# Second block: the 31 taps of one channel tile of a depthwise convolution, on VectorE or on GpSimd

## The chip, the core and the metric

The kernel is one program on one core of a Trainium2 chip. The metric is the device time of one launch in microseconds (us): lower is better. Engines are named as the profile names them: PE (TensorE), PEld (its weight loads), DVE (VectorE), ACT (ScalarE), POOL (GpSimd), SP (SyncE, which issues most DMAs).

## The reference, cut to what matters

The model has a first block and a second block of two layers, for 256 tokens of width 1024. A layer of the second block is a mixer, a cross-attention to a memory of 256 tokens, and a feed-forward part (dense in the first layer, a mixture of eight experts in the second). The mixer:

```python
z = xn @ w_in
a_val, a_gate, b_gate, c_gate, b_in, c_z = jnp.split(z, splits, axis=-1)
ya = a_val * jax.nn.sigmoid(a_gate)                        # 384 channels
ya = causal_depthwise_conv(ya, conv_a_w) + conv_a_b        # 31 taps
ya = jax.nn.silu(layernorm(ya, ln_a_g, ln_a_b))
yb = b_gate * causal_depthwise_conv(c_gate * b_in, conv_b_w)   # 3 taps
c_u, c_v = jnp.split(jax.nn.gelu(c_z), 2, axis=-1)
c_v = layernorm(c_v, ln_c_g, ln_c_b)
yc = chunk_spatial_gate(c_u, c_v, gmlp_ws, gmlp_b)
y = rmsnorm of jnp.concatenate([ya, yb, yc]) by groups of 64
return y @ w_mix_out
```

The change concerns the second line of `ya`: per channel, 31 shifted copies of a row of 256 tokens, each times one weight, are added to a bias.

## The kernel before

Channels lie on the 128 partitions, tokens along the row. Branch A has 384 channels, so three tiles t = 0, 1, 2 of 128x256 in `yap` (with 30 zeros before each row); their convolution is summed in `y8[:, t]`. Both are views of the tile `arena`, which is the name that the profile shows. `vb` holds v of branch C, `prod` and `cg` serve branch B.

**Weights.** SP loads each weight slot of 128x2048 float32 into `raw`. ACT rounds it to `whi` (L612, in `ahead`), DVE computes the rest `wlo = raw - whi` (L1578, in `ahead`), and PE makes three products of each (L1045, 48 matmuls per group of 256 columns). `whi` and `wlo` have three buffers, so a slot's rounding waits until PE has used the slot three before. In `group(g)` ACT and DVE first split up to two slots ahead, then wait for PE's product of g. The order of all work is written out by hand in each engine's program; no planner sets it.

**The mixer of a layer, by engine.** PE multiplies the groups mixa (three), mix_bg, mix_bgcg, then turns the memory (L1303), mix_cg, mix_bin, mix_binuv, mix_u, mix_v. Then come small products between the groups of keys (xk0 to xk3) and values (xv0 to xv3) of the memory: the means of v (L1319 to L1321), keys 0, the sums of squares of v, keys 1, v turned (L1331), keys 2, the spatial weights turned (L1337), the spatial product (L1345), keys 3, then the means of branch A (L1352, which waits at L1350 for all 93 taps), values 0, its squares (L1357), values 1, the squares of the whole mix (L1363), values 2, and so on.

DVE runs the taps between its splits. `conv_a(n)` issues the next n of a list ordered by k, then t. The first of each tile is a TENSOR_SCALAR (L1922), the others are a SCALAR_TENSOR_TENSOR (L1926), which reads a shifted row of `yap` and `y8`, both in SBUF, and writes `y8`. A tap waits for the tap of its own tile before it, three places back. Nine taps follow the splits of each of mix_bg, mix_bgcg, mix_cg, mix_bin, mix_u and mix_v; nine more follow `memory_low("xk", 0)`, then 12, 12 and 6 follow the low parts of keys 1, 2 and 3 (93 in all). In between lie:

- L1932, L1934: the memory scaled by its norm; L1942: the memory's low part, eight instructions, with one input in PSUM and one in SBUF
- L1947, L1952: the products for branch B, with one input in PSUM
- L1967: v centred, once L1321 has given its mean, and ACT's square of it (L882), behind which ACT splits xk2
- L1972, L1974, L1977: v normed and scaled; PE's L1331 waits for L1977
- `memory_low` (its instruction is L1596): the low parts of keys and values
- after the last tap: L1991 to L1994 (branch B), L2002 and L2003 (branch C), then L2007 (branch A centred, by the means of L1352), L2011, L2013. ACT squares (L898), applies silu (L905) and squares everything (L909), for which PE's L1363 waits.

POOL has little to do in this stretch. Per layer it clears the pads (L566, L567), loads the memory (L570), waits for PE to have turned it, loads the spatial weights `wsl` (L573), waits for them and clears a corner (L576, which PE's L1337 needs), waits for L1977 and loads the biases `gb` (L583), which DVE's L2002 needs.

Of the kernel before, what the change touches and what calls it, by code (L numbers as in the profile page):

```python
# [15 lines left out]
T = 256  # L16
# [170 lines left out]
def build_program(nc, w, onehot, out, bias_dram):  # L187
# [51 lines left out]
    with ctx:  # L239
# [235 lines left out]
        def _(pool):  # L475
# [88 lines left out]
            for l in range(2):  # L564
                pool.wait_ge(sem("dve_read"), reads_at[stage_groups[("down", "down2")[l]][-1]])
                link(pool.memset(yap[:, :, 0:30], 0.0))  # L566
                pool.memset(prod[:, :, 0:2], 0.0).then_inc(sem("mix_padded"), 1)  # L567
# [4 lines left out]
                pool.wait_ge(sem("mem_turned"), 4 * (l + 1))  # L572
                pool.dma_start(wsl, w["gmlp_ws_2"][l].rearrange("g i j -> i g j")).then_inc(sem("ws_landed"), 16)  # L573
                pool.wait_ge(sem("ws_landed"), 16 * (l + 1))
                pool.wait_ge(sem("mix_padded"), l + 1)
                pool.memset(wsl[0:64, :, 64:128], 0.0).then_inc(sem("ws_masked"), 1)  # L576
# [463 lines left out]
        def _(pe):  # L1040
# [250 lines left out]
            for l in range(2):  # L1291
# [58 lines left out]
                pe.wait_ge(sem("conv_taps"), 93 * (l + 1))  # L1350
# [211 lines left out]
        def _(dve):  # L1562
# [343 lines left out]
            for l in range(2):  # L1906
                norm(f"mix{l}", xT, lambda c: col("norm_mix_g_2", DC * l + c))
                dve.wait_ge(sem("mix_padded"), l + 1)
# [7 lines left out]
                taps = [(k, t) for k in range(TAPS_A) for t in range(3)]  # L1916
                done = {"k": 0}

                def conv_a(n):
                    for k, t in taps[done["k"]:done["k"] + n]:  # L1920
                        if k == 0:
                            ins = dve.tensor_scalar(y8[:, t], yap[:, t, 0:T], vec[:, aw + t:aw + t + 1], vec[:, ab + t:ab + t + 1],  # L1922
                                                    ALU.mult, ALU.add)
                        else:
                            dve.wait_ge(sem("conv_taps"), 93 * l + 3 * k + t - 2)
                            ins = dve.scalar_tensor_tensor(y8[:, t], yap[:, t, k:k + T], vec[:, aw + 3 * k + t:aw + 3 * k + t + 1],  # L1926
                                                           y8[:, t], ALU.mult, ALU.add)
                        ins.then_inc(sem("conv_taps"), 1)
                    done["k"] += n
# [5 lines left out]
                for stage in ("mix_bg", "mix_bgcg", "mix_cg"):  # L1935
                    ahead_of(stage_groups[f"{stage}{l}"][0])
                    conv_a(9)
# [10 lines left out]
                conv_a(9)  # L1948
# [4 lines left out]
                for stage in ("mix_u", "mix_v"):  # L1953
                    ahead_of(stage_groups[f"{stage}{l}"][0])
                    conv_a(9)
# [14 lines left out]
                conv_a(9)  # L1970
# [8 lines left out]
                conv_a(12)  # L1979
                memory_low("xk", 2)  # L1980
                conv_a(12)
                memory_low("xk", 3)
                conv_a(93 - done["k"])
                dve.wait_ge(sem("conv_taps"), 93 * (l + 1))
# [255 lines left out]
```

## Time and profile before

| | us |
|---|---|
| median of three runs (2370.57 to 2370.88) | 2370.84 |
| the profiled execution | 2369.96 |
| its span, first to last instruction | 2368.2 |
| PE busy | 2232.5 |
| DVE busy | 1749.6 |
| ACT busy | 1328.3 |
| POOL busy | 75.8 |

The mean granted clock of TensorE is 0.973 of its full speed. Times below are from the span's start. The mixer of the first layer lies between about 599 and 735 us, that of the second between about 1050 and 1187 us; the code of both is the same. In a timeline a row gives the start, the time of the group, the engine, the line and operation, output and input, and in brackets the engine's idle time ahead of it and what ended it.

### The profile page before, as it was taken

The page shows a single profiled execution, that of the slowest core. Times are in us where ns is not written, and L with a number is a line of the kernel's source. Part 1 is how long each engine was busy: PE and PEld are TensorE (multiplying, and loading weights), DVE is VectorE, ACT ScalarE, POOL GpSimd, SP SyncE. Part 2 cuts the span into 40 slices and gives each one's busy share as a digit, 9 for nine tenths or more (in the row PEclk, how much of TensorE's full clock was granted, in tenths as well). Part 3 has the DMA queues.
Part 4 walks back from the last instruction along what each step waited for, and adds up shares of the span by engine and source line. Part 5 has one row for each costly group of instructions (what it writes and reads, how often), then busy time and mean ns, then how long its engine had stood idle before and what let it go on. Part 6 is the DMA issues. An engine that isn't in the chain of part 4 may idle for free.

```text
span 2368.2 us, 35018 instructions
## 1 busy us (share of the span) xinstructions
PE 2232.5 (94%) x13975; PEld 1997.1 (84%) x13975; DVE 1749.6 (74%) x1928; ACT 1328.3 (56%) x1288; POOL 75.8 (3%) x159
## 2 busy tenths in 40 slices
PE   6999998999989899999897799999999999999997
PEld 4988987999978899999787688888888888888886
DVE  5668855884795555558864588888888888888885
ACT  3564433653534444345343576777676777777674
POOL 5011200000000000000000000000000000000000
PEclk9999999999999999999899799999999999999998
DMA  9637746756544356555342499989999999989992
GB/s 274 181 122 228 238 156 167 197 175 187 160 134 143 90 144 188 172 177 164 114 163 82 159 374 338 372 321 371 336 367 347 347 374 335 369 318 374 333 368 110
DMA packets 415499, 566.51 MB, mean 239 GB/s; under 512 B 17098, under 2 KB 268212, under 8 KB 415344
## 3 DMA queue, kind: packets, MB, share of 16 engines
q1 hardware_dynamic: 410160, 556.31, 68.8%
q0 software_dynamic: 4896, 6.89, 1.2%
q8 instruction: 121, 1.98, 0.3%
q10 hardware_dynamic: 288, 1.05, 0.1%
q14 instruction: 34, 0.28, 0.0%
HBM read 562.37 MB, written 1.84 MB: 238 GB/s over the span
## 4 chain that ended last, share of the span: by engine, by line
PE 80%; DVE 9%; ACT 4%; issue 2%; DMA 0%; ACTq 0%; SPq 0%; DVEq 0%
PE pair L1045 58%; PE misc L1045 13%; DVE wlo L1578 2%; DVE arena L1926 2%; PE misc L1451 1%; PE pair L1462 1%; PE misc L1486 1%; ACT whi L612 1%; PE misc L1115 1%; PE misc L1230 1%; PE misc L1099 0%; PE misc L1363 0%; DVE rt L1603 0%; DMA raw<-in_w_up_dram 0%; PE misc L1271 0%
## 5 line engine op out<-in xcount | busy, mean ns | idle before, releaser
L2122 DVE TENSOR_TENSOR wlo<-raw,whi 128x2048 fp32r<-128x2048 f32 x338 | 769.8, 2289 | 124.4 <-ACT whi L976 123.4
L976 ACT CAST whi<-raw 128x2048 fp32r<-128x2048 f32 x338 | 646.9, 1917 | 202.8 <-PE misc L1045 101.2
L1045 PE MATMUL pair<-hh,whi 128*128 128x256 f32 x1840 | 532.4, 289 | 24.0 <-DVE hl L1596 19.6
L1578 DVE TENSOR_TENSOR wlo<-raw,whi 128x2048 fp32r<-128x2048 f32 (+1 forms) x174 | 385.1, 2215 | 210.6 <-ACT whi L612 209.9
L1045 PE MATMUL pair<-hl,whi 128*128 128x256 f32 x1840 | 526.5, 286 | 0.0
L1045 PE MATMUL pair<-hh,wlo 128*128 128x256 f32 x1840 | 526.2, 286 | 0.0
L1045 PE MATMUL pair<-whi,oph 128*128 128x512 f32 (+1 forms) x1024 | 394.4, 385 | 4.8 <-DVE wlo L2122 3.1
L1045 PE MATMUL pair<-wlo,oph 128*128 128x512 f32 (+1 forms) x1024 | 386.6, 378 | 0.0
L1045 PE MATMUL pair<-whi,opl 128*128 128x512 f32 (+1 forms) x1024 | 385.9, 377 | 0.0
L1045 PEld LDWEIGHTS pair<-hh,whi 128*128 128x128 f32 x1840 | 359.3, 195 | 30.9 <-issue 26.4
L612 ACT CAST whi<-raw 128x2048 fp32r<-128x2048 f32 (+1 forms) x174 | 320.6, 1843 | 87.4 <-PE pair L1045 72.9
L1045 PEld LDWEIGHTS pair<-hl,whi 128*128 128x128 f32 x1840 | 359.5, 195 | 0.3
L1045 PEld LDWEIGHTS pair<-hh,wlo 128*128 128x128 f32 x1840 | 359.2, 195 | 0.0
L1045 PEld LDWEIGHTS pair<-whi,oph 128*128 128x128 f32 x1024 | 193.7, 189 | 42.6 <-DVE wlo L2122 6.1
L1045 PEld LDWEIGHTS pair<-wlo,oph 128*128 128x128 f32 x1024 | 193.4, 189 | 36.2
L1045 PEld LDWEIGHTS pair<-whi,opl 128*128 128x128 f32 x1024 | 193.9, 189 | 33.4
L1045 PE MATMUL pair<-oph,whi 128*128 128x256 f32 x672 | 194.1, 289 | 5.0 <-issue 3.0
L1045 PE MATMUL pair<-opl,whi 128*128 128x256 f32 x672 | 190.8, 284 | 0.0
L1045 PE MATMUL pair<-oph,wlo 128*128 128x256 f32 x672 | 190.8, 284 | 0.0
L1045 PE MATMUL misc<-whi,oph 128*128 128x512 f32 x448 | 176.1, 393 | 0.0
L1045 PE MATMUL misc<-wlo,oph 128*128 128x512 f32 x448 | 174.5, 389 | 0.0
L1045 PE MATMUL misc<-whi,opl 128*128 128x512 f32 x448 | 174.3, 389 | 0.0
(418 smaller groups left out, 2502.1 us busy)
## 6 DMA issues: line engine op xcount, KB each, us to landing
raw<-in_moe_w_gate_dram SPq DMA_DIRECT2D x114, 1024.0 KB, 7.0
raw<-in_moe_w_up_dram SPq DMA_DIRECT2D x112, 1024.0 KB, 7.0
raw<-in_moe_w_down_dram SPq DMA_DIRECT2D x112, 1024.0 KB, 6.8
raw<-in_w_in_dram SPq DMA_DIRECT2D x38, 1024.0 KB, 5.3
raw<-in_w_mod_dram SPq DMA_DIRECT2D x24, 1024.0 KB, 5.9
raw<-in_w_up_dram SPq DMA_DIRECT2D x44, 512.0 KB, 5.2
raw<-in_w_xkv_dram SPq DMA_DIRECT2D x16, 1024.0 KB, 5.5
raw<-in_ffn_w_gate_dram SPq DMA_DIRECT2D x22, 512.0 KB, 3.9
```

The lines of the kernel that those rows point to most:

```text
L612: act.copy(whi[:, i_ % SPLIT, 0:size], raw[:, raw_of(n), 0:size]).then_inc(sem("hi_ready"), 1)
L976: act.copy(whi[:, q, :], raw[:, r, :]).then_inc(sem("hi_ready"), 1)
L1045: ins = pe.matmul(out_, lhs, rhs, start=start and i == 0, stop=stop and i == 2)
L1115: ins = pe.matmul(misc[:, 0, 0:T], ones[:], squares[:, c], start=(c == 0), stop=(c == DC - 1))
L1230: ins = pe.matmul(misc[:, h % 2, i * P:(i + 1) * P], q[:, qb * P:(qb + 1) * P], k[:, kb * P:(kb + 1) * P], start=True, stop=True)
L1451: ins = pe.matmul(misc[:, 1 - half, c * P:(c + 1) * P], hn_tok[:, i, f:f + P], place[:, i, :], start=(i == 0), stop=(i == 1))
L1462: ins = pe.matmul(banks[:, r, m * T:(m + 1) * T], ye[:, f:f + P], comb_t[:, cb], start=True, stop=True)
L1486: ins = pe.transpose(misc[:, bank, c * P:(c + 1) * P], sh[:, j % 2, c * P:(c + 1) * P], ident[:])
L1578: dve.tensor_tensor(wlo[:, i_ % SPLIT, 0:size], raw[:, raw_of(n), 0:size], whi[:, i_ % SPLIT, 0:size].bitcast(F32), ALU.subtract).then_inc ...
L1926: ins = dve.scalar_tensor_tensor(y8[:, t], yap[:, t, k:k + T], vec[:, aw + 3 * k + t:aw + 3 * k + t + 1], y8[:, t], ALU.mult, ALU.add)
L2122: dve.tensor_tensor(wlo[:, q, :], raw[:, r, :], whi[:, q, :].bitcast(F32), ALU.subtract).then_inc(sem("lo_ready"), 1)
```

## The change

Tile 2 of the convolution leaves DVE. DVE's list then holds 62 taps instead of 93 (`range(2)`), each waiting for the tap two places back, and its nine, nine, ..., 12, 12, 6 become six, six, ..., 8, 8, 4. POOL computes tile 2: for k = 0 a tensor_scalar into `y8[:, 2]`, for each k from 1 to 30 a tensor_scalar (multiply) into a scratch row and a tensor_tensor that adds it to `y8[:, 2]`, 61 instructions per layer, each waiting for the one before it through `link`. The scratch row lies in a part of `raw` that holds no weights at that time. POOL's load of `wsl` stands ahead of tap 10, its wait and the clearing ahead of tap 14; the loads of `gb` stay behind the last tap. PE's means of branch A wait for DVE's 62 taps and for POOL. The semaphore `mix_padded` is replaced by `pool_mixed`, which counts two per layer.

```diff
@@ POOL
-                pool.memset(prod[:, :, 0:2], 0.0).then_inc(sem("mix_padded"), 1)
+                pool.memset(prod[:, :, 0:2], 0.0).then_inc(sem("pool_mixed"), 1)
...
-                pool.wait_ge(sem("mem_turned"), 4 * (l + 1))
-                pool.dma_start(wsl, w["gmlp_ws_2"][l].rearrange("g i j -> i g j")).then_inc(sem("ws_landed"), 16)
-                pool.wait_ge(sem("ws_landed"), 16 * (l + 1))
-                pool.wait_ge(sem("mix_padded"), l + 1)
-                pool.memset(wsl[0:64, :, 64:128], 0.0).then_inc(sem("ws_masked"), 1)
+                aw, ab = VROW["conv_a_w_2"] + 93 * l, VROW["conv_a_b_2"] + 3 * l
+                pool.wait_ge(sem("dve_read"), reads_at[stage_groups[f"mixa{l}"][2]])
+                link(pool.tensor_scalar(y8[:, 2], yap[:, 2, 0:T], vec[:, aw + 2:aw + 3], vec[:, ab + 2:ab + 3], ALU.mult, ALU.add))
+                for k in range(1, TAPS_A):
+                    if k == 10:
+                        pool.wait_ge(sem("mem_turned"), 4 * (l + 1))
+                        pool.dma_start(wsl, w["gmlp_ws_2"][l].rearrange("g i j -> i g j")).then_inc(sem("ws_landed"), 16)
+                    if k == 14:
+                        pool.wait_ge(sem("ws_landed"), 16 * (l + 1))
+                        pool.wait_ge(sem("pool_mixed"), 2 * l + 1)
+                        pool.memset(wsl[0:64, :, 64:128], 0.0).then_inc(sem("ws_masked"), 1)
+                    tap = spare[:, 0:T]
+                    link(pool.tensor_scalar(tap, yap[:, 2, k:k + T], vec[:, aw + 3 * k + 2:aw + 3 * k + 3], None, ALU.mult))
+                    ins = pool.tensor_tensor(y8[:, 2], y8[:, 2], tap, ALU.add)
+                    if k < TAPS_A - 1:
+                        link(ins)
+                ins.then_inc(sem("pool_mixed"), 1)
@@ PE
-                pe.wait_ge(sem("conv_taps"), 93 * (l + 1))
+                pe.wait_ge(sem("conv_taps"), 2 * TAPS_A * (l + 1))
+                pe.wait_ge(sem("pool_mixed"), 2 * (l + 1))
@@ DVE
-                taps = [(k, t) for k in range(TAPS_A) for t in range(3)]
+                taps = [(k, t) for k in range(TAPS_A) for t in range(2)]
...
-                            dve.wait_ge(sem("conv_taps"), 93 * l + 3 * k + t - 2)
+                            dve.wait_ge(sem("conv_taps"), 2 * TAPS_A * l + 2 * k + t - 1)
...
-                    conv_a(9)
+                    conv_a(6)
...
-                conv_a(12)
+                conv_a(8)
...
-                conv_a(93 - done["k"])
-                dve.wait_ge(sem("conv_taps"), 93 * (l + 1))
+                conv_a(2 * TAPS_A - done["k"])
+                dve.wait_ge(sem("conv_taps"), 2 * TAPS_A * (l + 1))
```

## Rows read from the trace of the kernel before

**Rows 1.** The stages of both mixers: us, busy (instructions), PE's clock, DMA share, GB/s

```profile
625.00:650.00 25.00, 25.00 (x213) 25.00 (x212) 24.88 (x46) 13.57 (x19) 1.25 (x2) 1.00 0.49 148
...
600.00:760.00 160.00, 147.53 (x1119) 142.54 (x1119) 125.57 (x204) 74.61 (x88) 4.64 (x8) 0.95 0.45 143
1050.00:1212.00 162.00, 149.69 (x1131) 145.05 (x1132) 127.24 (x208) 77.03 (x92) 5.56 (x9) 0.94 0.45 144
```

**Rows 2.** Waits from 600 to 730 us: total, times, longest

```profile
PE misc L1352 <- DVE arena L1926: 3.8, 1, 3.8
...
PE misc L1331 <- DVE arena L1977: 3.0, 1, 3.0
```

**Rows 3.** Timeline of DVE in the first mixer

```profile
623.45 0.17 DVE L1932 RECIPROCAL tiny<-tiny 128x2 f32<-128x2 f32 x1 [3.26 <-ACT tiny L847]
...
638.71 3.65 DVE L1926 SCALAR_TENSOR_TENSOR arena<-arena,vec 128x256 f32<-128x256 f32 x9
642.28 3.22 DVE L1942 SCALAR_TENSOR_TENSOR opl<-misc,vec,oph 128x256 fp32r<-128x256 f32 x8
...
651.77 2.28 DVE L1578 TENSOR_TENSOR wlo<-raw,whi 128x2048 fp32r<-128x2048 f32 x1
...
665.84 1.08 DVE L1967 SCALAR_TENSOR_TENSOR arena<-misc,arena 128x256 f32<-128x256 f32 x3
669.63 2.29 DVE L1578 TENSOR_TENSOR wlo<-raw,whi 128x2048 fp32r<-128x2048 f32 x1 [2.71 <-ACT whi L612]
671.84 0.68 DVE L1596 TENSOR_TENSOR opl<-pair,oph 128x512 fp32r<-128x512 f32 x1
...
697.80 0.69 DVE L1596 TENSOR_TENSOR opl<-pair,oph 128x512 fp32r<-128x512 f32 x1 [0.53 <-ACT oph L873]
698.41 2.46 DVE L1926 SCALAR_TENSOR_TENSOR arena<-arena,vec 128x256 f32<-128x256 f32 x6
```

**Rows 4.** Timeline of ACT in the first mixer

```profile
655.57 0.60 ACT L867 ACTIVATE arena<-pair 128x512 f32<-128x512 f32 x1 [3.19 <-PE pair L1045]
...
671.48 0.47 ACT L885 ACTIVATE rt<-misc,consts 128x256 f32<-128x256 f32 x1
```

**Rows 5.** Chain of waits, keys 2 and values 2: start, us, what

```profile
681.53 6.69 PE pair L1045 x48
...
726.39 5.75 PE pair L1045 x48
```

**Rows 6.** PE alone by stretch: us, busy (instructions), clock, DMA share, GB/s

```profile
676.00:680.00 4.00, 0.97 (x9) 1.00 0.14 46
680.00:684.00 4.00, 3.98 (x21) 0.57 0.20 48
```

**Rows 7.** Timeline of POOL in the first mixer

```profile
632.81 0.89 POOL L573 DMA_DIRECT2D work<-in_gmlp_ws_dram  x1 [27.80 <-PE misc L1303]
639.09 0.36 POOL L576 MEMSET work<- 64x320 f32 x1 [5.39 <-DMA work<-in_gmlp_ws_dram]
680.26 2.66 POOL L583 DMA_DIRECT2D arena<-in_gmlp_b_dram  x5 [40.81 <-DVE arena L1977]
```

**Rows 8.** Timeline of POOL at the kernel's start, beside DVE's L1635

```profile
26.66 0.68 POOL L538 TENSOR_SCALAR_AFFINE_SELECT spread<-spread 32x512 f32<-32x512 f32 x1
27.41 0.68 POOL L540 TENSOR_SCALAR_AFFINE_SELECT spread<-spread 32x512 f32<-32x512 f32 x1
```

**Rows 9.** L1635 from 14 to 25 us, then from 25: ns min/median/max

```profile
L1635 DVE SCALAR_TENSOR_TENSOR opf<-raw,cact,opf x14: 483/485/486, 14.8 to 24.4; 128x256 f32<-128x256 f32 x14
...
L1635 DVE SCALAR_TENSOR_TENSOR opf<-raw,cact,opf x7: 711/712/777, 25.4 to 29.9; 128x256 f32<-128x256 f32 x7
```

**Rows 10.** Instructions of POOL alone, at the start

```profile
0.81 0.21 POOL L485 MEMSET ident<- 128x128 f32 x1 [0.29 <-POOLq L2236]
1.26 0.28 POOL L486 TENSOR_SCALAR_AFFINE_SELECT ident<-ident 128x128 f32<-128x128 f32 x1 [0.24 <-POOL ident L485]
...
24.64 0.53 POOL L535 MEMSET spread<- 128x512 f32 x1
```

More of the change, by code:

```diff
@@ L1907, in _ @@
                 norm(f"mix{l}", xT, lambda c: col("norm_mix_g_2", DC * l + c))
-                dve.wait_ge(sem("mix_padded"), l + 1)
+                dve.wait_ge(sem("pool_mixed"), 2 * l + 1)
                 for t, g in enumerate(stage_groups[f"mixa{l}"]):
@@ L1947, in _ @@
                 dve.tensor_tensor(prod[:, 0:2, 2:2 + T], ps, cg[:, 0:2, :], ALU.mult).then_inc(sem("dve_read"), 1)
-                conv_a(9)
+                conv_a(6)
                 g = stage_groups[f"mix_binuv{l}"][0]
@@ L1954, in _ @@
                     ahead_of(stage_groups[f"{stage}{l}"][0])
-                    conv_a(9)
+                    conv_a(6)
                 def memory_low(stage, j):
@@ L1969, in _ @@
                 memory_low("xk", 0)
-                conv_a(9)
+                conv_a(6)
                 dve.wait_ge(sem("root_ready"), ROOTS.index(f"v{l}") + 1)
@@ L1978, in _ @@
                 memory_low("xk", 1)
-                conv_a(12)
+                conv_a(8)
                 memory_low("xk", 2)
-                conv_a(12)
+                conv_a(8)
                 memory_low("xk", 3)
-                conv_a(93 - done["k"])
-                dve.wait_ge(sem("conv_taps"), 93 * (l + 1))
+                conv_a(2 * TAPS_A - done["k"])
+                dve.wait_ge(sem("conv_taps"), 2 * TAPS_A * (l + 1))
                 bw = lambda k, t: col("conv_b_w_2", 6 * t + 3 * l + k)
```

## The prediction

> **What bounds the kernel now.** I read the stages first, then the waits inside the mixer, then the engines' timelines. Of 160 us around the first mixer PE is busy for 147.5, and the second mixer is its copy to within 0.5% on DVE [rows 1]; all terms are worked out in the first and doubled. From 625 to 650 us PE is busy for 25.00 us and DVE for 24.88 [rows 1]: both are full, since a group costs DVE one split of 2.28 us and nine taps of 3.65 [rows 3], and costs PE 5.75 [rows 5]. DVE alone can't shorten that part. What it can give back is in PE's stalls: 3.0 us for L1977 and 3.8 for the last tap [rows 2], behind which comes a tail of dependent steps to L1363. A stall also costs clock: after the first one (0.97 us busy in 4) the granted clock averaged 0.57 over the next 4 us, so it was mostly at 1.2 GHz instead of 2.4 [rows 6], and keys 2 took 6.69 us where values 2 took 5.75 [rows 5].
>
> **Removed from DVE.** Nine taps span 642.28 - 638.71 = 3.57 us, 0.40 each [rows 3]. Of 31 removed taps per layer, 18 stood ahead of L1967, three between it and L1977, two in the last batch behind keys 3: 23 x 0.40 = 9.1 us on the path. The other eight, behind keys 1 and 2, are worth nothing: DVE already waited 0.53 us for ACT's copy of keys 3 [rows 3]. A tap now waits for the one two places back; two spacings are 0.80 us, room for an instruction of this kind, which takes 0.49 at most [rows 9], so this costs nothing.
>
> **Added on POOL.** 61 instructions per layer, each waiting for the last. No row shows either kind. POOL's rate is (0.53 - 0.21) / 384 elements = 0.83 ns [rows 10], so 0.21 us for 256; a reading instruction of 128x128 took 0.28 [rows 10], hence 0.39 for 256, and 0.07 from one to the next (27.41 - 26.66 - 0.68) [rows 8]. For the tensor_tensor I bound the time in which it streams: 0.21 if both inputs flow together, 0.43 if one after the other (512 elements, as in rows 8), 0.86 at twice that. I take 0.54, the middle of the outer ends and a quarter above the row of equal reads, since alternating between inputs can only add to that row. The Trainium skill (GPSIMD Engine Reference, "Performance versus the Vector engine") gives about 2.6 cycles an element, an estimate of 0.55 us, which would leave the sum where it is. A tap alone then costs 0.39 + 0.71 + 2 x 0.07 = 1.24 us, 31 of them 38 us, from 623.45 - 3.26 = 620.2, where mixa's third product is read [rows 3]: done by 659, against the last tap of DVE at 698.41 + 2.46 = 700.9 [rows 3].
>
> **The price is contention.** At the kernel's start DVE's L1635, a scalar_tensor_tensor on two SBUF inputs like a tap, ran 14 times in 0.485 us with POOL issuing DMAs or clearing, and seven times in 0.712 beside POOL's reading instructions [rows 9]; those started every 0.75 us [rows 8]. DVE's streaming is (2.28 - 0.68) / 1536 = 1.04 ns an element [rows 3], 0.27 us for 256. POOL 0.43 + DVE 0.27 = 0.70 of the 0.75: they take turns, with 0.05 for handing over. So a tap beside a POOL tensor_scalar starts every 0.21 + 0.27 + 0.05 = 0.53 us, beside a tensor_tensor every 0.54 + 0.27 + 0.05 = 0.86, instead of 0.40: +0.13 and +0.46, **0.30 us on average** per turn.
>
> How many turns? From 620.2 POOL has 3.3 us in which DVE waits [rows 3], five instructions, and one more until 625. L1942 (3.2 us, one input in PSUM [rows 3]) leaves it five, the products for branch B and L1967 two. Of 61, 48 must take turns. Ahead of L1967 DVE has seven splits and 36 taps, 43 instructions with room for one of POOL's behind each; less two first taps (one input) and three in which POOL issues `wsl` (0.89 us) or waits for it [rows 7]: 38. Of the ten left, four fit into the 2.7 us in which DVE waits for ACT's split of xk2 [rows 3], three take turns with the six taps ahead of L1972, and the last run beside L1972 and L1977. Sum per layer: 41 x 0.30 = 12.3, less 9.1, **+3.2 us**. It all reaches the end, since from L1967 on one thing follows another: L1967, ACT's L882, its split of xk2, DVE's split, the six taps, L1972, L1977, PE's L1331, keys 2, keys 3, the last taps, L1352 and the tail, which is as long as before. PE's stall for L1977 grows, with no more low clock than one such stall has.
>
> **Moved or hidden.** Splits come late by at most 2 to 3 us; that of mix_v was ready at 654.05 against a start at 655.5 [rows 3, 4], so PE may wait about 1 us there, hidden by L1967 being later still. `wsl` is issued at tap 10, some 3 us later than at 632.8, lands 5.4 us on [rows 7], is cleared by 646 or so and needed when keys 2 end, 688.2 [rows 5]. `gb` stands behind POOL's last tap (about 679) but also behind L1977 (now about 684), 2.66 us of issue [rows 7], and is needed by L2002, behind the last tap and twelve instructions of branch B: nothing. The router's load follows it, for a product behind the whole layer. SP's queue isn't touched. PE's second wait: nothing.
>
> Sum: 2369.96 + 2 x 3.2 = 2376.4 for an execution like the profiled one; the median stands 0.9 us above it, so **2377**.
>
> **Rivals.**
> 1. No contention in this stretch (DVE's taps overlap one another, L1635 did not). Then L1967 is 2 us earlier, held by PE's mean, and L1977 is held by the root at 671.95 [rows 4] and the xk2 chain: the stall of 3.0 falls to 0.3. With two fewer last taps (0.8) and most of 0.94 of clock [rows 5], 4.4 us per layer: **2362**, faster. Against it stand rows 9. It decides where a turn costs under 0.13 us. Chance 0.17.
> 2. Turns cost what the row of equal reads says, tensor_tensor at 0.43: +0.35 and +0.13, 0.24 on average. 41 x 0.24 - 9.1 = +0.7 per layer: **2372**, within 0.2%. For it: it is a row. Against: two inputs. With values up to my own, the band up to 2375.6: chance 0.33.
> 3. The instruction blocks whole, dispatch included: 0.39 and 0.71 in place of the streams give turns of 0.71 and 1.03, +0.47 on average, 41 x 0.47 - 9.1 = +10 per layer: **2391**, slower; the upper end of 0.86 gives the same. Rows 8 speak against it: whole blocking, 0.68 + 0.485, would be a period of 1.16, not 0.75. The Trainium skill (SBUF — State Buffer, "Who interferes with whom") has the shared pair taken for the whole instruction and the other engine fully blocked; the trace agrees that they take turns, not that it lasts the whole instruction. Chance 0.10.
> 4. DVE keeps the port between its dense taps and POOL starves: a POOL tap of 3 us instead of 1.5 ends at 713, 12 us behind the last tap: **2395**. Chance 0.03. That POOL finishes late for another reason is in it.
>
> **How the numbers follow.** A measurement of this kernel tells about 0.2%, 4.7 us, from no change. My forecast, from 2375.6 to 2383, has 0.37. Slower is 0.37 + 0.10 + 0.03 = 0.50, same 0.33, faster 0.17. The forecast's own range is 2375 to 2383. The range of 8 in 10 takes in rival 2, most of rival 1 down to 2363, and reaches to 2388, leaving out rival 4 and most of 3.
>
> **What the profile would show.** Right: 120 instructions of L1926 instead of 180, starting about every 0.7 us in mix_bg to mix_v and every 0.40 after POOL's last; POOL's tensor_scalars and tensor_tensors in step with them; L1967 near 671, L1977 near 683; PE's wait at L1331 at about 4 us, at L1352 about 3.0, for DVE and not POOL; POOL's last tap near 679. Wrong: taps at 0.40 beside POOL's (rival 1), POOL ending near 659, or L1352 released by POOL (rival 4).

## The result, and the profile after

| | before | changed kernel |
|---|---|---|
| median of all runs, us | 2369.48 | 2376.18 |
| lowest to highest | 2364.03 to 2370.88 | 2371.17 to 2383.86 |
| the profiled execution | 2369.96 | 2377.47 |

The changed kernel is slower: ratio 1.0032, 95% interval 1.0021 to 1.0042. The forecast was 2377, with "slower" as the likeliest of the three. One execution of e8 below took 2524 us at a granted clock of 0.83; such slow executions are left out of the ratios.

From the first page, the engines' busy time in the changed kernel:

```profile
PE 2236.2 (94%) x13975; PEld 1999.1 (84%) x13975; DVE 1755.1 (74%) x1866; ACT 1328.2 (56%) x1288; POOL 225.2 (9%) x281
```

DVE has 62 instructions fewer than before and is busy for 5.5 us longer. That line alone says that what was taken from DVE was not given back. The stages, to be held against [rows 1]:

```profile
625.00:650.00 25.00, 25.00 (x212) 25.00 (x211) 25.00 (x37) 13.53 (x18) 23.11 (x20) 1.00 0.56 172
...
600.00:760.00 160.00, 145.48 (x1099) 140.41 (x1098) 125.07 (x165) 73.08 (x84) 79.40 (x69) 0.94 0.44 142
1050.00:1212.00 162.00, 143.00 (x1077) 137.45 (x1078) 129.62 (x177) 75.65 (x93) 80.33 (x70) 0.94 0.44 141
```

From 625 to 650 us DVE still has no free moment, with 37 instructions where it had 46. PE's waits from 600 to 730 us, which answer to [rows 2]:

```profile
PE misc L1344 <- DVE arena L1991: 5.8, 1, 5.8
PE misc L1366 <- DVE arena L1940: 3.2, 1, 3.2
```

L1344 is the old L1331 and L1366 the old L1352. The wait for v normed grew from 3.0 to 5.8 us; the wait for the taps is where it was. The timeline of DVE, which answers to [rows 3] (L1940 are the taps, L1981 the old L1967, L1986 to L1991 the old L1972 to L1977):

```profile
620.88 0.17 DVE L1946 RECIPROCAL tiny<-tiny 128x2 f32<-128x2 f32 x1 [3.26 <-ACT tiny L860]
...
631.01 3.78 DVE L1940 SCALAR_TENSOR_TENSOR arena<-arena,vec 128x256 f32<-128x256 f32 x6
...
640.63 3.21 DVE L1956 SCALAR_TENSOR_TENSOR opl<-misc,vec,oph 128x256 fp32r<-128x256 f32 x8
...
658.75 2.81 DVE L1592 TENSOR_TENSOR wlo<-raw,whi 128x2048 fp32r<-128x2048 f32 x1
...
665.28 1.07 DVE L1981 SCALAR_TENSOR_TENSOR arena<-misc,arena 128x256 f32<-128x256 f32 x3
...
677.13 2.01 DVE L1988 SCALAR_TENSOR_TENSOR arena<-arena,vec,rt 128x256 f32<-128x256 f32 x3
679.18 1.37 DVE L1991 TENSOR_SCALAR arena<-arena,vec 128x256 f32<-128x256 f32 x3
...
699.08 1.81 DVE L1940 SCALAR_TENSOR_TENSOR arena<-arena,vec 128x256 f32<-128x256 f32 x4
```

Six taps take 3.78 us where nine took 3.65 [rows 3]: a group of taps lasts as long as before, with a third of them gone. The row of the eight instructions with one input in PSUM is untouched, 3.21 us for 3.22. The executions start their mixers at different times (620.88 and 623.45), so I count from that first row. L1981 begins 44.40 us behind it (before 42.39), L1991 58.30 (before 55.64), and the last tap ends at 80.01 (before 77.42). The timeline of POOL (L584 multiplies, L585 adds):

```profile
618.38 0.93 POOL L584 TENSOR_SCALAR raw<-arena,vec 128x256 f32<-128x256 f32 x1
619.39 0.74 POOL L585 TENSOR_TENSOR arena<-arena,raw 128x256 f32<-128x256 f32 x1
...
632.72 0.97 POOL L584 TENSOR_SCALAR raw<-arena,vec 128x256 f32<-128x256 f32 x1
633.77 0.74 POOL L585 TENSOR_TENSOR arena<-arena,raw 128x256 f32<-128x256 f32 x1
634.61 3.09 POOL L584 TENSOR_SCALAR raw<-arena,vec 128x256 f32<-128x256 f32 x1
...
657.06 0.36 POOL L582 MEMSET work<- 64x320 f32 x1
```

The first two rows lie in DVE's idle time, so they are POOL's own durations: 0.93 and 0.74 us. The row of 3.09 lies over a split of DVE, from 634.71 on: POOL stood still for its 2.28 us. One line each for DVE's taps and for POOL's two instructions, from the view of one source line (ns: shortest, median, longest; both layers together):

```profile
L1940 DVE SCALAR_TENSOR_TENSOR arena<-arena,vec x120: 467/693/1036, 626.0 to 1158.4; 128x256 f32<-128x256 f32 x120
...
L584 POOL TENSOR_SCALAR raw<-arena,vec x60: 922/977/3363, 618.4 to 1153.5; 128x256 f32<-128x256 f32 x60
L585 POOL TENSOR_TENSOR arena<-arena,raw x60: 721/739/2537, 619.4 to 1156.7; 128x256 f32<-128x256 f32 x60
```

**Where the 7.5 us between the two profiled executions went.** I measure a mixer from the reciprocal on `tiny` to the reciprocal for the last root of the layer. In the first layer these are the following rows, of the kernel before and of the changed kernel:

```profile
726.93 1.75 DVE L2018 RECIPROCAL rt<-rt 128x256 f32<-128x256 f32 x1 [1.29 <-ACT rt L912]
```

```profile
726.96 1.75 DVE L2032 RECIPROCAL rt<-rt 128x256 f32<-128x256 f32 x1 [1.29 <-ACT rt L925]
```

So the first mixer went from 103.48 to 106.08 us, and by the same rows the second from 103.01 to 106.15: **+5.7 us for both**. The stretch between the two mixers, whose code the change does not touch, went from 347.8 to 351.9 us (+4.1), the part ahead of the first mixer from 623.45 to 620.88 (-2.6), the rest by +0.2. The stretch between differs by TensorE's clock: with 2594 matmuls in both profiles PE is busy in it for 328.8 us instead of 324.9, at a mean granted clock of 0.97 instead of 0.98. Two windows of PE alone (us, busy, granted clock, DMA share, GB/s), before and changed:

```profile
735.00:742.00 7.00, 7.00 (x59) 1.00 0.06 19
805.00:812.00 7.00, 6.93 (x53) 1.00 0.27 67
```

```profile
735.00:742.00 7.00, 7.00 (x47) 0.76 0.05 18
805.00:812.00 7.00, 4.84 (x28) 0.76 0.54 150
```

In the changed kernel parts of both windows ran at 1.2 GHz, where before all of them had 2.4. Each kernel has one profiled execution, and executions of one kernel differ too: the 29 of the kernel before beside which e6 ran took 2364.9 to 2376.7 us at clocks from 0.974 to 0.966, and the part ahead of the first mixer, which but for POOL's first instructions is the same in all kernels of this study, took 619.6 to 624.9. So what a kernel does to the total is read from the medians, and where one execution has its low clock is not thereby shown for the others.

### The profile page after: what moved, and what is told of

Same layout as the page of the kernel before. It is cut to its first block, busy times and chain, and to the rows that moved or that the text cites. A ratio compares the mean times of both kernels' runs of the same rounds, so it can differ in the third digit from the quotient of the medians.

```text
span 2375.7 us, 35082 instructions
## 1 busy us (share of the span) xinstructions
PE 2236.2 (94%) x13975; PEld 1999.1 (84%) x13975; DVE 1755.1 (74%) x1866; ACT 1328.2 (56%) x1288; POOL 225.2 (9%) x281
## 4 chain that ended last, share of the span: by engine, by line
PE 80%; DVE 9%; ACT 3%; issue 2%; DMA 0%; SPq 0%; ACTq 0%; DVEq 0%
PE pair L1058 58%; PE misc L1058 13%; DVE arena L1940 2%; DVE wlo L1592 2%; PE misc L1465 1%; PE pair L1476 1%; PE misc L1500 1%; ACT whi L625 1%; PE misc L1128 1%; PE misc L1243 1%; PE misc L1112 0%; PE misc L1377 0%; DVE rt L1617 0%; DMA raw<-in_w_up_dram 0%; PE misc L1284 0%
```

## The experiments

Each mixer below is measured by the same two rows, the stretch between them likewise. "To last tap" is the part of a mixer up to the end of DVE's last tap. "Held" is what the 60 scalar_tensor_tensor taps of the first layer (90 in kernels derived from the one before, 89 in e6 and e7) took beyond 0.476 us each, their duration with POOL quiet.

| kernel | ratio to before (95%) | mixers, us | to last tap, us | between, us | held, us |
|---|---|---|---|---|---|
| before | | 103.5, 103.0 | 77.4, 77.1 | 347.8 | 0.2 |
| changed | 1.0032 (1.0021 to 1.0042) | 106.1, 106.2 | 80.0, 80.0 | 351.9 | 11.9 |
| e1 POOL does the first tap alone | 0.9958 (0.9946 to 0.9970) | 97.0, 98.4 | 72.3, 72.3 | 347.3 | 0.1 |
| e2 POOL only writes | 0.9982 (0.9967 to 0.9997) | 99.2, 99.1 | 73.1, 73.1 | 351.9 | -0.1 |
| e3 before, POOL reads beside | 1.0179 (1.0156 to 1.0201) | 119.9, 119.6 | 93.8, 93.5 | 351.9 | 12.4 |
| e4 before, reordered | 0.9974 (0.9961 to 0.9987) | 98.7, 98.7 | 74.0, 74.0 | 349.9 | 0.1 |
| e5 shorter multiply | 1.0018 (1.0008 to 1.0029) | 104.1, 105.1 | 79.4, 79.0 | 347.3 | 9.5 |
| e6 two taps in the gap | 1.0025 (1.0012 to 1.0038) | 102.7, 102.7 | 76.6, 76.7 | 351.9 | 0 |
| e7 e4 and e6 | 0.9956 (0.9941 to 0.9972) | 98.0, 98.0 | 73.3, 73.3 | 349.7 | 0 |
| e8 changed, reordered | 1.0010 (0.9999 to 1.0021) | 101.8, 101.8 | 77.1, 77.1 | 349.7 | 13.0 |
| e9 delay of 0.5 | 1.0022 (1.0010 to 1.0034) | 103.7, 105.0 | 77.8, 78.9 | 347.6 | -0.1 |
| e10 delay of 1.3 | 1.0044 (1.0030 to 1.0058) | 105.9, 105.2 | 79.8, 79.1 | 349.5 | -0.1 |
| e11 only the additions | 1.0025 (1.0013 to 1.0036) | 104.0, 105.0 | 79.3, 78.9 | 347.3 | 8.1 |
| e12 only the multiplications | 0.9956 (0.9942 to 0.9971) | 97.0, 98.4 | 72.3, 72.3 | 347.4 | 3.1 |

Behind the last tap a mixer takes 24.7 us or 25.9 to 26.2, with and without POOL's taps. The rows of the same reciprocal show where the two differ: before it waits 1.29 us for ACT's root (726.93, above), in e1 not at all, and PE's clock ahead of it averaged 0.72 from 721 to 727 us before and 1.00 from 712.2 to 717 in e1. This 1.4 us is clock and not DVE's work, so DVE's part is read up to the last tap.

```profile
716.79 1.74 DVE L2027 RECIPROCAL rt<-rt 128x256 f32<-128x256 f32 x1
```

My theory: the change takes work from DVE and gives the time back because DVE and POOL take turns at SBUF. Its rival: nothing is lost by turns, and what is slower comes from waits or from POOL's place in the order.

**e1.** The changed kernel; of POOL's taps only the first is left, so the third tile's sum is left out.

```diff
-                    link(pool.tensor_scalar(tap, yap[:, 2, k:k + T], ...))
-                    ins = pool.tensor_tensor(y8[:, 2], y8[:, 2], tap, ALU.add)
```

> Edit: the changed kernel with POOL's taps 1 to 30 of tile 2 left out (the output lacks them); DVE, PE and ACT as in the changed kernel. Theory (turns on the shared read path cost DVE what the removed taps save): without POOL's reads every tap of DVE starts 0.40 us after the last, PE's stall ahead of L1331 falls to about 0.3 us, and the kernel is about 4.4 us per layer faster than before, ratio about 0.996. Rival (the stretch is held by PE and the chain behind the last tap, and contention doesn't matter): as the changed kernel, ratio about 1.003, with the stall ahead of L1331 unchanged.

Ratio 0.9958, as expected: without POOL the 62 taps make the kernel 10 us faster. It is also the most that the move could ever have given, and it is less than the taps removed. DVE's timeline and PE's longest and shortest waits:

```profile
636.00 3.22 DVE L1951 SCALAR_TENSOR_TENSOR opl<-misc,vec,oph 128x256 fp32r<-128x256 f32 x8 [0.80 <-ACT oph L868]
...
648.77 2.29 DVE L1587 TENSOR_TENSOR wlo<-raw,whi 128x2048 fp32r<-128x2048 f32 x1 [0.99 <-ACT whi L620]
...
689.82 0.69 DVE L1605 TENSOR_TENSOR opl<-pair,oph 128x512 fp32r<-128x512 f32 x1 [2.11 <-ACT oph L881]
```

```profile
PE misc L1361 <- DVE arena L1935: 3.0, 1, 3.0
...
PE misc L1339 <- DVE arena L1986: 0.3, 1, 0.3
```

Of 31 x 0.397 = 12.3 us taken from DVE, about half turned into waits of this kind (9.8 us from the first tap to the last, where before had 3.2; 2.7 of both are the wait for the split of xk2 [rows 3]). Up to the last tap the mixers became 5.1 and 4.8 us shorter; in all it is 6.5 and 4.6, and the 1.4 us more of the first layer are the clock behind the last tap. PE's wait for v fell from 3.0 to 0.3; ACT and PE then set the pace.

**e2.** POOL's 60 instructions become as many clearings of about the same length, which read nothing; the third tile's sum is left out.

```diff
-                    link(pool.tensor_scalar(tap, ...))
-                    ins = pool.tensor_tensor(y8[:, 2], y8[:, 2], tap, ALU.add)
+                    link(pool.memset(spare[:, 0:896], 0.0))
+                    ins = pool.memset(spare[:, 0:896], 0.0)
```

> Edit: the changed kernel with each of POOL's 60 instructions per layer for taps 1 to 30 replaced by a memset of 128x896 (about 0.84 us by POOL's rate of 0.83 ns an element), with the same waits between them (the output lacks these taps). POOL is as busy and sends as many semaphores, but reads nothing. Theory (DVE's second SBUF input and POOL's reads take turns): DVE's taps at 0.40 us, time within 2 us of the kernel without POOL's taps, ratio about 0.996. Rival (any work of POOL, its writes or its semaphores slow DVE): taps at 0.6 us or more, ratio near 1.003.

The taps beside it, then beside nothing in e1, from the view of one line:

```profile
L1940 DVE SCALAR_TENSOR_TENSOR arena<-arena,vec x120: 465/474/483, 626.1 to 1143.2; 128x256 f32<-128x256 f32 x120
```

```profile
L1935 DVE SCALAR_TENSOR_TENSOR arena<-arena,vec x120: 472/478/488, 624.4 to 1136.0; 128x256 f32<-128x256 f32 x120
```

POOL's writes hold no scalar_tensor_tensor. That a busy POOL is enough to slow the taps falls; its reading is needed. They do hold DVE's tensor_scalar, which has one input, in SBUF:

```profile
619.75 2.71 DVE L1948 TENSOR_SCALAR work<-work,tiny 128x1024 f32<-128x1024 f32 x2
```

The same two took 1.42 us before and in e1. The two first taps (L1936) span 1.56 us for 0.73 in e1, and L1991 1.67 for 0.88, so 2.9 us a layer beside clearings. Most of it falls into waits: up to the last tap the mixer lasts 73.1 us for e1's 72.3. The ratio (0.9982) missed the 0.996: the mixers are 4.3 and 3.9 us shorter than before's, and the stretch between them is 4.1 longer.

**e3.** The kernel before, all 93 taps on DVE, and POOL does its 61 instructions besides, into scratch; no engine waits for their result.

```diff
+                link(pool.tensor_scalar(spare[:, T:2 * T], yap[:, 2, 0:T], ...))
+                for k in range(1, TAPS_A):
...
+                    link(pool.tensor_scalar(tap, yap[:, 2, k:k + T], ...))
+                    ins = pool.tensor_tensor(spare[:, T:2 * T], spare[:, T:2 * T], tap, ALU.add)
```

> Edit: the kernel before, all 93 taps on DVE, and in addition POOL does the 61 instructions per layer into a scratch row that nobody waits for. Theory: this is the cost of contention alone, unmixed with what was removed. In the changed kernel 62 taps took 36.9 us instead of 24.6, and splits and L1974 to L1977 some 2 us more; here the same reads meet more DVE work, so 12 to 15 us per layer, of which nearly all reaches the end: 24 to 30 us slower than before, ratio 1.010 to 1.013. Rival (the changed kernel lost its time by waiting for POOL's late last tap, or in PE's extra wait): ratio 1.000 to 1.002, since nobody waits for POOL here.

The taps are held for 12.4 us a layer, just as in the changed kernel, and this is contention by itself, since nothing waits for POOL. The mixers grew by 16.4 and 16.5 us, the total by 42, against 24 to 30 expected. In the first mixer the taps are 12.2 us of it, the other held instructions (splits, tensor_scalars, L1974's kind) 3.3 where I had expected some 2, and a wait 0.5. Some 8 us of the profiled execution lie outside the mixers (4.1 between them and 4.0 behind), for which I had no term. PE's waits show two places where DVE is late, of which the first was none before:

```profile
PE pair L1055 <- DVE arena L1957: 4.9, 1, 4.9
PE misc L1341 <- DVE arena L1987: 4.8, 1, 4.8
```

**e4.** The kernel before, with DVE's last taps ahead of the low part of keys 3. This asks what the order alone gives, without POOL.

```diff
                 memory_low("xk", 2)
-                conv_a(12)
-                memory_low("xk", 3)
                 conv_a(93 - done["k"])
...
+                memory_low("xk", 3)
                 memory_low("xv", 0)
```

> Edit: the kernel before with the last six taps issued ahead of the low part of keys 3, and that low part (with the split ahead of it) moved behind L2007. Theory (the tail from the last tap to L1363 is a chain of DVE): the last tap ends at about 697.4 instead of 700.9, PE's stall of 3.8 us ahead of L1352 falls to about 0.5, the tail keeps its length, and the low part of keys 3 fits into the 2.7 us in which DVE waits for ACT: about 3 us per layer, ratio about 0.9975. Rival (the moved low part holds up values 1, which need its buffer): what is won ahead of L1352 is lost ahead of values 1, ratio 1.000.

```profile
PE misc L1331 <- DVE arena L1977: 3.0, 1, 3.0
PE misc L1357 <- ACT arena L898: 2.6, 1, 2.6
PE misc L1363 <- ACT work L909: 1.3, 1, 1.3
...
PE misc L1352 <- DVE arena L1926: 0.5, 1, 0.5
```

The mixers are 4.8 and 4.3 us shorter, 3.4 and 3.1 of it up to the last tap, and the ratio is the expected one, with 2.1 us more between the mixers. The wait of 3.8 us for the last tap [rows 2] was one of order, not of DVE's load.

**e5.** The changed kernel with a second operation in POOL's multiply, the addition of a zero column. In the changed kernel POOL's first tap, which has two operations, took 0.54 us, and its one-operation multiply 0.93.

```diff
-                    link(pool.tensor_scalar(tap, yap[:, 2, k:k + T], vec[...], None, ALU.mult))
+                    link(pool.tensor_scalar(tap, yap[:, 2, k:k + T], vec[...], consts[:, 2:3], ALU.mult, ALU.add))
```

> Edit: the changed kernel with POOL's multiply of taps 1 to 30 given a second operation (add of a zero column). In the changed kernel the multiply alone took 0.93 us and the first tap's multiply-and-add 0.54, so a tap of POOL shrinks from about 1.85 to 1.46 us with the same reads. Theory (each reading instruction of POOL costs DVE's next tap a fixed delay, 0.49 us for the tensor_tensor and 0.22 for the tensor_scalar, and in the changed kernel one tap in three went free): now hardly any tap goes free while POOL works, so more delay falls ahead of L1977, though POOL ends sooner: the mixer gets 2 to 4 us longer per layer than in the changed kernel, ratio 1.004 to 1.006. Rival (the delay goes with how long POOL is busy, or POOL's late end matters): the mixer gets shorter, ratio 1.002 or less.

A miss, in the sign against the changed kernel: I expected it slower than the change, and it is not (1.0018 against 1.0032, with intervals that overlap); its mixers are shorter by 2.0 and 1.1 us, up to the last tap by 0.6 and 1.0. That is the rival's number; its reason, a price by POOL's busy time, is tried in e11 and e12.

```profile
L1940 DVE SCALAR_TENSOR_TENSOR arena<-arena,vec x120: 467/548/1025, 628.5 to 1153.5; 128x256 f32<-128x256 f32 x120
...
L584 POOL TENSOR_SCALAR raw<-arena,vec,consts x60: 556/849/2732, 621.0 to 1143.9; 128x256 f32<-128x256 f32 x60
```

Alone the multiply takes 0.56 us, beside DVE's taps 0.85: POOL now waits where DVE had waited. In one layer 30 taps of DVE are held, 15 beside an addition by 0.48 us and 15 beside a multiplication by 0.14; in the changed kernel it is 17 by 0.49 and 19 by 0.20. So the price goes by the kind of POOL's instruction more than by its duration (0.93 us of multiplying cost 0.20, 0.74 of adding 0.49), and a shorter instruction does not raise the number of turns: in both kernels DVE makes three taps while POOL makes one.

**e6.** The kernel before; POOL makes the first two taps of the third tile in the 3.3 us in which DVE waits ahead of the mixer [rows 3], DVE the other 91.

```diff
+                link(pool.tensor_scalar(y8[:, 2], yap[:, 2, 0:T], ..., ALU.mult, ALU.add))
+                link(pool.tensor_scalar(spare[:, 0:T], yap[:, 2, 1:1 + T], ..., None, ALU.mult))
+                pool.tensor_tensor(y8[:, 2], y8[:, 2], spare[:, 0:T], ALU.add).then_inc(sem("pool_mixed"), 1)
...
+                taps = [(k, t) for k in range(TAPS_A) for t in range(3) if t < 2 or k >= 2]
```

> Edit: the kernel before, with only taps 0 and 1 of tile 2 on POOL, in the 3.3 us in which DVE waits for the memory's norm (91 taps on DVE, the first batch seven instead of nine). Theory (POOL's taps cost only where DVE reads two SBUF inputs at the same time): nothing is paid, two taps of 0.40 us are saved ahead of L1967, the mixer is 0.8 us shorter per layer, ratio about 0.999. Rival (a tap on POOL always costs more than it saves): the mixer is as long as before or longer.

By the mixers it is as expected: 0.8 and 0.3 us shorter, no tap held, PE's wait for v 2.3 us instead of 3.0. By the total it is a miss: 1.0025 where 0.999 was expected. The stretch between the mixers took 351.9 us instead of 347.8, as in the changed kernel and in e2 and e3.

**e7.** The kernel before with the edits of e4 and e6 together.

```diff
                 memory_low("xk", 2)
-                conv_a(12)
-                memory_low("xk", 3)
-                conv_a(93 - done["k"])
+                conv_a(91 - done["k"])
```

> Edit: the reordered kernel before (last six taps ahead of the low part of keys 3, that one behind L2007) with taps 0 and 1 of tile 2 on POOL as well. Theory: the two gains add, since one lies ahead of L1977 and the other behind it: mixer 4.6 + 0.8 = 5.4 us shorter per layer than before, ratio 0.996 to 0.997. Rival (they share the same slack): as the reordered kernel, ratio about 0.9975.

2358.19 us, ratio 0.9956 (0.9941 to 0.9972). **This is the fastest complete kernel of the study**, and POOL makes none of its taps in it while DVE's run. Most of the gain is e4's order; that e7 beats e4 lies within their intervals.

**e8.** The changed kernel with e4's order.

```diff
-                memory_low("xk", 3)
                 conv_a(2 * TAPS_A - done["k"])
...
+                memory_low("xk", 3)
                 memory_low("xv", 0)
```

> Edit: the changed kernel with the same reordering (the last four taps ahead of the low part of keys 3, that one behind L2007). In the changed kernel POOL's last add ended 1.4 us ahead of DVE's last tap. DVE's last tap now moves 3.4 us forward. Theory: POOL becomes the one that PE waits for at its means of branch A, or ties with it within 0.5 us, and of the 4.6 us per layer that the reordering gave the kernel before, 2 to 4 are left: ratio 1.000 to 1.001. Rival (POOL is far from being the bound): all of it, PE released by DVE, ratio 0.9995 or less.

The mixers are 4.3 and 4.4 us shorter than in the changed kernel, nearly as much as the order gave in e4 (up to the last tap 2.9, there 3.4 and 3.1). In the total it comes to 1.0010, the upper end of what was expected.

```profile
694.53 7.42 DVE L1940 SCALAR_TENSOR_TENSOR arena<-arena,vec 128x256 f32<-128x256 f32 x12
```

```profile
700.53 0.74 POOL L585 TENSOR_TENSOR arena<-arena,raw 128x256 f32<-128x256 f32 x1
```

PE waited 0.2 us, for DVE's last tap (end 701.95) and not for POOL's (701.27): a tie but for 0.7 us, so the expected change of releaser did not come. In the mixers the rival came true, nearly all of the gain with DVE as releaser; only the total is as my theory had it, and 4.9 us of the profiled execution lie behind the second mixer (1195.6 us for the changed kernel's 1190.7).

**e9 and e10.** The kernel before with one more instruction in DVE's program, ahead of L1972: a clearing of 512 and of 1,536 elements a row. It adds a known delay; the rest of the program is as before.

```diff
                 conv_a(9)
+                link(dve.memset(spare[:, 0:512], 0.0))
                 dve.wait_ge(sem("root_ready"), ROOTS.index(f"v{l}") + 1)
```

> The kernel before with one more VectorE instruction per layer, a memset of 512 elements a row behind the tenth tap of the keys' conv, ahead of L1972. Theory (the mixer's time and the placement of TensorE's low-clock stretches behind it are two separate terms): the mixers grow by 0.3 to 0.6 us each, and the total by 0.6 to 1.2 us (ratio 1.0003 to 1.0005) if the stretch between the mixers stays at the 347.8 us of before, or by 4 to 6 us (1.002) if it takes the 349.8 or 351.9 us that the changed kernel and the exchange of two taps showed. Rival (what the code between the mixers takes depends on where the work stands, not on when it runs): 347.8 us between the mixers and a ratio of 1.0003 to 1.0005.

> The same with 1,536 elements. Both theories have the mixers grow by 1.2 to 1.8 us each, so 2.4 to 3.6 us by them alone (1.0010 to 1.0015). By the theory of two terms the stretch between the mixers may be 347.8, 349.8 or 351.9 us, and the total 2.4 to 8 us above before; by the rival it stays at 347.8.

```profile
676.46 0.48 DVE L1971 MEMSET raw<- 128x512 f32 x1
```

```profile
674.72 1.34 DVE L1971 MEMSET raw<- 128x1536 f32 x1 [0.27 <-issue]
```

The instructions of both layers last 1.0 and 2.7 us, and the medians are 3.96 and 9.33 us above the 2369.27 of before (by the ratios 5 and 10). The rival's 1.0003 to 1.0005 for e9 is excluded. My own theory was right in that the total goes up by several times the delay, and wrong on the place: in e9 the stretch between the mixers stayed at 347.6, and in the profiled execution 2.0 us lie in the second mixer and 2.1 behind it. PE alone from the end of the second mixer on, in the kernel before and in e9:

```profile
1178.00:1300.00 122.00, 107.10 (x825) 0.99 0.37 128
```

```profile
1180.00:1305.00 125.00, 111.52 (x829) 0.93 0.38 126
```

The clock of that stretch fell from 0.99 to 0.93. In e10 the mixers grew by 2.4 and 2.2 us, more than the 1.34 of the instruction, and the stretch between by 1.8. Its profiled execution (2374.86) is one of the faster ones, so it doesn't show where the median's 9 us lie. A delay of about a microsecond in a mixer comes with several us elsewhere, of which the profile of e9 shows low clock as a part, at places that I can't foretell. Of the 2.0 us by which the second mixer of e9 grew, 0.5 is the instruction and 1.0 a longer wait for ACT's copy of keys 3 (1.21 us for 0.24), behind a stretch in which PE's clock averaged 0.50 and 0.77 (1132 to 1136 and 1136 to 1140 us) where before had 0.74 and 1.00. What sets these places stays open.

**e11 and e12.** The changed kernel in which POOL makes only its additions, then only its multiplications; in e12 too the third tile is left without its sum.

```diff
-                    link(pool.tensor_scalar(tap, yap[:, 2, k:k + T], ...))
```

```diff
-                    ins = pool.tensor_tensor(y8[:, 2], y8[:, 2], tap, ALU.add)
```

> The changed kernel in which GpSimd makes only the 30 additions of a layer and not the multiplications (the third tile's result is another). Theory (each addition holds a VectorE tap for 0.48 us, each multiplication for 0.2 us or less): the additions follow each other every 0.8 us instead of every 1.9 us, GpSimd is done some 45 us sooner, and while it runs nearly every second VectorE tap takes 0.96 us; 30 additions by 0.48 us are at most 14 us a layer, less what falls into VectorE's waits, so 9 to 13 us in the taps: the mixers last 103 to 109 us (changed kernel 106.1). Rival (the price is per microsecond in which GpSimd is busy, 61 instructions or 30): busy time falls by more than half, the taps' extra falls from 12.3 to about 6 us, and the mixers last 99 to 101 us.

> The changed kernel in which GpSimd makes only the multiplications of a layer and not the 30 additions. Theory (0.2 us or less for each): 31 by 0.2 us are at most 6 us in the taps, so the mixers last 99 to 101 us and the total is 8 to 13 us below the changed kernel's (ratio 0.996 to 0.999 of before). Rival (a price by busy time, of which the multiplications have 1.7 times what the additions have): the taps' extra stays at 7 to 8 us and above that of the run with the additions alone.

```profile
L1939 DVE SCALAR_TENSOR_TENSOR arena<-arena,vec x120: 465/482/1194, 631.3 to 1154.4; 128x256 f32<-128x256 f32 x120
```

```profile
L1939 DVE SCALAR_TENSOR_TENSOR arena<-arena,vec x120: 469/476/702, 628.3 to 1139.7; 128x256 f32<-128x256 f32 x120
```

With additions alone 16 taps of a layer are held, by 0.50 us each (8.1 us, just under the 9 to 13 expected), and the mixers last 104.0 and 105.0 us, within the 103 to 109. With multiplications alone 15 are held by 0.20 us (3.1 us), and the mixers last 97.0 and 98.4, exactly as in e1, below my 99 to 101; the total is 18 us below the changed kernel's by the ratios, where I had expected 8 to 13. Together they make 11.1 of the changed kernel's 11.9 us. The rival, a price by POOL's busy time, falls: the multiplications keep POOL busier (84 us against 60) and cost less than half as much. That e12 equals e1 shows something that I had not counted: the first 3 us of contention a layer are free, since they fall into the idle time that the removed taps leave on DVE (its waits from the first tap to the last are 6.5 us in e12, 9.8 in e1).

## Why the prediction was right, and where its steps were off

The sign, the mechanism (turns between DVE's and POOL's reads take back what the removed taps give) and the total (2377 against 2376.18) were right. Of the two terms of the sum neither was: they were too large by about the same amount.

**Removed from DVE: 9.1 us on the path, measured 5.1 and 4.8 up to the last tap.** e1 is this term by itself. I counted 23 taps as being on the path because DVE was full from 625 to 650 us. It was full, but PE was too, and ACT has splits and copies with little room: without the 31 taps DVE waits 6.6 us longer for them. Rival 1 had this floor almost right: it took PE's wait for v to fall to 0.3, which e1 shows to the tenth, and gave 4.4 us a layer for a move without contention.

**The price of a turn: 0.30 us forecast, measured 0.33.** Held were 17 taps by 0.49 us and 19 by 0.20, in all 36 taps and 11.9 us; I had forecast +0.46 and +0.13 for the two kinds. The row that this came from, a scalar_tensor_tensor of the same size with and without POOL's reads [rows 9], was worth more than every other argument. The tensor_tensor's stream, which I had to choose between 0.21 and 0.86, was well placed at 0.54: from a tap beside an addition to the next tap 0.88 us pass, where the forecast had 0.86 (beside a multiplication 0.62 for 0.53). Rival 2 (0.43) asked for +0.35 and +0.13 and falls with the 0.49; rival 3, whole instructions one behind the other, asked for +0.63 and +0.31 and falls too. The Trainium skill (SBUF — State Buffer, "SBUF: two separate sides") has whichever of the two starts first take the shared pair for the whole instruction, the other engine fully blocked. The trace agrees in part:

```profile
633.83 0.95 DVE L1940 SCALAR_TENSOR_TENSOR arena<-arena,vec 128x256 f32<-128x256 f32 x1
```

```profile
632.82 0.69 DVE L1940 SCALAR_TENSOR_TENSOR arena<-arena,vec 128x256 f32<-128x256 f32 x1
```

The first met the addition of 633.77 and ended at 634.79, 0.28 us behind its end at 634.51. That is the 0.27 us which DVE needs to stream a tap (an estimate of the prediction), so it did wait to the addition's end, as the others beside an addition did. The second met the multiplication of 632.72 and ended at 633.51, 0.18 us ahead of its end at 633.69, so it was not blocked for that whole instruction. And the multiplication of 634.61 began 0.10 us ahead of a split of DVE and yet stood for all of it (3.09 us). What falls is rival 3's price, not every form of blocking.

**How many turns: 41 by 679 us, measured 36 taps and some others by 699.** This step failed. I took a POOL tap alone at 1.24 us, with 0.39 for the multiply, from the affine_select of 0.28 us [rows 10]. It took 0.93, so a tap is 1.85 us with the gaps. I also gave POOL room behind each of DVE's instructions, splits included, and did not see that a POOL instruction that starts beside a split waits for its end: the rows of 2.2 to 3.4 us on POOL, about one for each split. So POOL's last tap ended at 699.43 and not near 679 (78.5 us behind the first reciprocal, forecast 55.6), 1.5 us ahead of DVE's own. Rival 4, POOL as the last to finish, was within that much of coming true, and I had given it 0.03. It also means that fewer turns lay ahead of L1967 (23 held taps, forecast 38 turns), which is 2.0 us late instead of the forecast 5, and more behind it: L1988 takes 2.01 us for 1.27 and L1991 1.37 for 0.88, two items that I had priced only as "the last run beside" them. PE's wait at L1344 is 5.8 us instead of the forecast 4, though L1991 is only 2.7 us late, because the wait of about 1 us that I had put ahead of mix_v did not come. The eight taps behind keys 1 and 2, which I had priced at nothing, paid for POOL's late taps. A smaller error is that I let instructions with one input go free, as I did the two first taps: that holds for an input in PSUM, but the tensor_scalars with one input in SBUF were held (L1948 1.90 us for 1.42, the first taps 0.93 for 0.73, L1991 as above), and e2 shows that POOL's writes alone do this.

**The sum.** Forecast 12.3 - 9.1 = +3.2 us a layer. Measured in the first layer up to the last tap: 5.1 us gained by the removal (72.3 us in e1 for 77.4). From e1 to the changed kernel the taps then take 11.9 us more and L1948, the first taps, L1988, L1991 and the splits together some 2.7, while DVE's waits shrink from 9.8 us to 3.3, so 6.5 us of the price fall into the idle time which the removal left. 11.9 + 2.7 - 6.5 - 5.1 = +3.0 for the +2.6 of the rows, so 0.4 is left over. In the second layer the mixer is +3.1, of it +2.9 up to the last tap. The two terms by themselves, 7.7 us lost and 5.1 gained where 12.3 and 9.1 were forecast, are both too large because the same slack takes from both.

**What else it said.** No wait for `wsl`: cleared at 657.06 (forecast 646 or so), needed at 688.7. The loads of `gb` came behind POOL's last tap and nobody is seen to wait for them. The wait at the old L1352 at 3.0, for DVE: 3.2, for DVE. The stall at v costs clock once, as before: keys 2 took 6.74 us in the chain of waits for 6.69 [rows 5]. But "no more low clock" held for that place only. The changed kernel's profile has 4.1 us more in code that the change does not touch, and 2.6 less ahead of it. I had no term for this and no row of before shows it. e6 and e9 show that such a shift is not the change's own: there a microsecond or less in a mixer came with a median 4 to 5 us higher. That the forecast met the median to 1 us is therefore in part luck; what the runs bear out is +5.7 us in the two mixers, against +6.4 forecast.

## What to carry to other kernels

To move a two-input vector operation to GpSimd as two instructions costs VectorE more than it saves when VectorE's neighbours read two SBUF inputs too: here 11.9 us of held taps and some 2.7 of other held instructions a layer for 12.3 us removed. Give GpSimd such work where VectorE waits (e6: no tap held, mixers 0.8 and 0.3 us shorter, though the total did not gain) or, as the row of L1956 suggests, where it reads PSUM. First look whether the wait is one of order: moving six taps ahead of a low part that was not due yet gave 3.1 to 3.4 us a layer up to the last tap without touching the load (e4). A price for sharing comes best from a row of the same instruction in the same trace with and without the neighbour, and the work removed is worth no more than the next engine's slack; in a kernel whose total shifts by several us with a delay of half a microsecond, compare the stretch that was changed and not the total alone.

## What the runs showed of the hardware that I had not expected

- GpSimd's tensor_scalar with one operation takes 0.93 us for 128x256 float32, with two operations 0.54 to 0.56; its tensor_tensor takes 0.74.
- A VectorE scalar_tensor_tensor with two SBUF inputs takes 0.96 us beside GpSimd's tensor_tensor and 0.68 beside its tensor_scalar (0.476 alone), 0.474 beside its memset. With one input in PSUM it is not held at all: eight of them in 3.21 us for 3.22.
- A VectorE tensor_scalar with its one input in SBUF is held even by GpSimd's memset: 128x1024 float32 takes 1.37 to 1.41 us beside it (e2) and 0.75 without.
- Beside a tensor_tensor the held tap ends 0.28 us behind it; beside the one-operation tensor_scalar it ends 0.18 us ahead of it.
- A GpSimd instruction that reads waits for the whole of a VectorE tensor_tensor of 2.28 us that it meets, even one that begins 0.10 us behind it, and takes up to 3.36 us; among dense taps of 0.48 us it keeps nearly its own pace (0.97 us for 0.93) and the taps pay.
- The code between the mixers, the same in all kernels, took 347.3 to 347.8 us in six profiles, 349.5 to 349.9 in four, and 351.9 in four, with TensorE at 1.2 GHz for longer in the changed kernel's 351.9 than in the 347.8 of before. The medians of e6 and e9 show that a change of a microsecond or less in a mixer can move the total by 4 to 5 us; by what rule is not shown.
